# A weight buffer of the expert down products lent to the gathered rows: two buffers in place of three

## The reference, cut to what matters

```
q = (xc @ w_q).reshape(128, 8, 2, 128)              # a block of 128 tokens
s = einsum("chsd,hskd->chsk", q, keys)              # 8 heads, 2 x 128 keys
... top 16 of each side, then the best 16 pairs: 16384 experts, 16 picked by each of 8 heads
e = i1 * 128 + i2;  g = softmax(best_s)
act = gelu(einsum("cd,chkd->chk", xc, u_tab[e]))
out = einsum("chk,chkd->cd", g * act, v_tab[e])
x = x + g_f * out
```

## Time and profile before

| | us |
|---|---|
| median of 3 runs (lowest, highest) | 2940.29 (2937.99, 2942.69) |
| the profiled execution, its own time | 2935.12 |
| its span, first to last instruction | 2933.3 |

### The profile page before, as it was taken

One profiled execution on the slowest core, in us unless ns is written; L12 is line 12 of the kernel. 1 busy time (PEld: TensorE's weight loads), 2 busy tenths in 40 slices (PEclk: granted clock), 3 DMA queues, 4 the chain that ended last, 5 costly groups with the idle time before them and its releaser, 6 DMA issues. The chain is left out here.

```text
span 2933.3 us, 36691 instructions
## 1 busy us (share of the span) xinstructions
PE 2632.2 (90%) x12550; PEld 2159.5 (74%) x12550; DVE 1990.6 (68%) x4287; ACT 1043.5 (36%) x2939; POOL 1349.4 (46%) x1076
## 2 busy tenths in 40 slices
PE   4789889999999999999965888999999999999992
PEld 2544558888888888888854766888888887878881
DVE  2356249998877866666674247998877775666667
ACT  3335142269878700000004423229888830000000
POOL 0000034455666666666550005365666674655562
PEclk7889999999999999999987989999999999999996
DMA  7247133799999999999991223599999999999995
GB/s 304 65 189 303 43 116 130 289 384 380 356 410 409 409 404 409 409 409 409 409 375 57 86 71 117 207 374 366 360 384 409 407 407 404 409 409 409 409 409 212
DMA packets 246591, 917.87 MB, mean 313 GB/s; under 512 B 27120, under 2 KB 32272, under 8 KB 239120
## 3 DMA queue, kind: packets, MB, share of 16 engines
q0 software_dynamic: 147456, 536.94, 46.6%
q1 hardware_dynamic: 94800, 374.54, 33.1%
q10 hardware_dynamic: 4160, 4.19, 0.4%
HBM read 909.27 MB, written 6.29 MB: 312 GB/s over the span
## 5 line engine op out<-in xcount | busy, mean ns | idle before, releaser
L1199 PE MATMUL exp_down<-peer_gates,all_ring 128*128 128x256 f32 x2720 | 613.3, 382 | 22.3 <-DMA all_ring<-in_peer_v 22.3
L1172 PE MATMUL exp_out<-peer_both,all_ring 128*128 128x256 f32 x2752 | 617.4, 380 | 9.4 <-DMA all_ring<-in_uT 5.7
L1199 PEld LDWEIGHTS exp_down<-peer_gates,all_ring 128*128 128x128 f32 x2720 | 508.0, 190 | 117.1 <-DMA all_ring<-in_peer_v 50.5
L1172 PEld LDWEIGHTS exp_out<-peer_both,all_ring 128*128 128x128 f32 x2752 | 515.9, 190 | 83.1 <-DMA all_ring<-in_uT 11.8
L1090 POOL DMA_INDIRECT all_xT<-in_u_rows,peer_eidx x278 | 350.4, 1260 | 169.6 <-DVE peer_dots L1548 115.6
L1555 DVE SCALAR_TENSOR_TENSOR peer_both<-all_xT,peer_dots,peer_both 128x1024 f32<-128x1024 f32 x226 | 290.3, 1285 | 147.7 <-DMA all_xT<-in_peer_v,peer_eidx 144.1
L1548 DVE CUSTOM_DVE_ANT_0 all_xT<-all_xT,peer_both 128x1024 f32<-128x1024 f32 x278 | 338.1, 1222 | 66.9 <-DMA all_xT<-in_u_rows,peer_eidx 65.2
L1063 POOL TENSOR_TENSOR ask_w_lo<-all_ring,ask_w_hi 128x1024 fp32r<-128x1024 f32 x22 | 52.5, 2390 | 675.4 <-ACT ask_w_hi L1227 675.4
L1090 POOL DMA_INDIRECT all_xT<-in_peer_v,peer_eidx x230 | 271.3, 1180 | 176.8 <-DVE peer_both L1555 144.3
L1199 PE MATMUL exp_down<-peer_gates,spare_ring 128*128 128x256 f32 x1376 | 315.6, 382 | 13.9 <-DMA spare_ring<-in_peer_v 13.9
L1299 ACT ACTIVATE spare_heavy<-all_iota_b,spare_index 128x128 f32<-128x128 bf16 x1024 | 314.2, 411 | 0.0
(11 more groups left out here) (288 smaller groups left out, 3843.0 us busy)
## 6 DMA issues: line engine op xcount, KB each, us to landing
all_ring<-in_uT SPq DMA_DIRECT2D x172, 512.0 KB, 6.8
all_ring<-in_peer_v SPq DMA_DIRECT2D x170, 512.0 KB, 6.8
mix_raw<-in_ada_tiles SPq DMA_DIRECT2D x48, 1024.0 KB, 9.6
spare_ring<-in_peer_v SPq DMA_DIRECT2D x86, 512.0 KB
spare_ring<-in_uT SPq DMA_DIRECT2D x84, 512.0 KB
all_ring<-in_w_peer_q SPq DMA_DIRECT2D x22, 512.0 KB, 3.7
all_ring<-in_w_gs_in SPq DMA_DIRECT2D x16, 512.0 KB, 3.7
all_ring<-in_w_in SPq DMA_DIRECT2D x12, 512.0 KB, 3.7
```

Of the source, the lines that this page charges most:

```text
L1172: mm = nc.tensor.matmul(outs[:, c % 2, 0:DENSE], raw[c % R][:, k, :], hd[:, k, :], start=(k == 0), stop=(k == KD - 1))
L1199: mm = nc.tensor.matmul(dn[:, m, :], raw[at % R][:, m, :], gates[:, :, c, :], start=(c == 0 and m % 2 == 0), stop=(c == NKEYS - 1), skip_g ...
```

## The change

The v chunks go through two buffers, `raw[0]` and `raw[1]`, and the third, `raw[2]` (`q.ring`), becomes a tenth place for gathered rows from slot NEAR + 2 = 264 on. The ups keep three buffers. The load of v chunk c waits for down c - 2, and the first two wait for the last up that read their buffer (`last_up` is 126, 127 and 125 for the three buffers). The first fetch into the new place waits for up 125.

```diff
-        R = len(raw)
+        R, DOWN = len(raw), 2
+        last_up = [max(range(j, NKEYS, R)) for j in range(R)]
...
+        rows += [raw[DOWN][:, :, :].rearrange("p k n -> p (k n)")]
+        spans += [(NEAR + 2, SLOTS)]
         rows += [x[:, :] for x in q.late]
...
-        ROW, OWN, PICKED_ROW = 4, 5 + len(EARLY), 6 + len(EARLY)
+        ROW, OWN, PICKED_ROW, RING_ROW = 4, 5 + len(EARLY), 6 + len(EARLY), 7 + len(EARLY)
...
-            for c in range(2 * NKEYS):
+            for c in range(NKEYS):
...
-                if c < NKEYS:
-                    sp.dma_start(raw[c % R][:, :, :], t["uT"][l][c]).then_inc(s_in[c % R], 16)
-                else:
-                    sp.dma_start(raw[c % R][:, :, :].rearrange("p k n -> p (k n)"),
-                                 v_dram[l * NKEYS + c - NKEYS]).then_inc(s_in[c % R], 16)
+                sp.dma_start(raw[c % R][:, :, :], t["uT"][l][c]).then_inc(s_in[c % R], 16)
+            for c in range(NKEYS):
+                j = c % DOWN
+                sp.wait_ge(s_mm, NKEYS + c - DOWN + 1 if c >= DOWN else last_up[j] + 1)
+                sp.dma_start(raw[j][:, :, :].rearrange("p k n -> p (k n)"), v_dram[l * NKEYS + c]).then_inc(s_in[j], 16)
...
+                elif j == RING_ROW:
+                    pool.wait_ge(s_mm, last_up[DOWN] + 1)
...
             def down(c):
-                at = NKEYS + c
-                pe.wait_ge(s_in[at % R], 16 * (at // R + 1))
+                j = c % DOWN
+                pe.wait_ge(s_in[j], 16 * (last_up[j] // R + 1 + c // DOWN + 1))
...
-                    mm = nc.tensor.matmul(dn[:, m, :], raw[at % R][:, m, :], gates[:, :, c, :],
+                    mm = nc.tensor.matmul(dn[:, m, :], raw[j][:, m, :], gates[:, :, c, :],
```

## The result

The changed kernel takes 3262.07 us (median of 5 runs, 3259.55 to 3268.61), the kernel before 2937.99 us beside it: 1.1106 times as long (95% interval 1.109 to 1.1121), 324 us slower. The forecast was 3205 us with a range of 3110 to 3245: the direction held, and the size did not. Of the mechanism one term was mis-sized, what a fall of TensorE's clock costs.

A forecast was written before the change was run, and what follows sets the result against it. The prediction took DMA bytes to bound the downs' stage; downs of 5.97 us beside rows, then 3.72 us, add 138 us a layer, 275 us on 2935.1, giving 3210, 3215 for the median, taken as 3205 us, range 3110 to 3245.

The forecast's parts named there:

- The bound of before: In the downs' stretch of the kernel before, DMA bytes bind: chunks and rows together take 402 of 408 GB/s.
- The landing stays: With two buffers, a v chunk beside rows still lands in about 7.0 us (median 6.8 before).
- Rival C: Downs beside rows: the landing shrinks to 5.0 us, a down takes 4.37 us, total 3029 us; chance 0.11.
- E: Downs beside rows: landing falls to 4.1 us, stage stays bound by bytes, not slower, 2931 us; chance 0.04.
- the estimate of 4.4 us: A chunk's landing beside rows by the Trainium skill's transfer cost at half the rate: 4.4 us, total near 2971 us.
- D: Downs beside rows: landing grows to 7.9 us, with clock falls a down takes 6.42 us, total 3241 us; chance 0.12.
- rival B: Downs beside rows: the clock stays at 2.4 GHz, a down takes 5.37 us, total 3160 us; chance 0.21.
- The clock: TensorE's clock falls after most pauses beside rows, 1.2 us each, 0.6 us a down, making 5.97 us a down.
- a bound, 3.5 us: Upper limit on a clock fall's cost per pair of downs: 7.07/2 = 3.5 us, all at half the clock.
- The rows: Gathered v rows beside the slowed chunks take 1.67 us each in place of 2.02, done near 1465 us.
- The tenth place: The new row place lets 10 rows be out in place of 9, keeping the queue full, with no other worth.
- near 0.85: Sign to look for: TensorE's granted clock well under 1.00 in the stretch with rows, and 1.00 after it.

The follow-up runs named there:

- e7: Kernel before with four chunk buffers for the downs and eight row places: 1.0021 of the kernel before, 6 us slower.
- e6: Kernel before, three chunk buffers kept, with a tenth row place from slot 290 on in freed gates memory: 1.0002 of the kernel before.
- e1: Changed kernel with 7 extra matmul calls on resident data after each second down while c < 80: 1.0816 of the kernel before, 3173 us.
- e11: Changed kernel without the gathers of v rows, two chunk buffers: 0.9934 of the kernel before, 2920 us.
- e3: Changed kernel with the tenth row place taken away, two chunk buffers, the third left empty: 1.1087 of the kernel before.
- e9: Kernel before, three chunk buffers and nine row places, with v chunks loaded in halves of 2 KB per partition: 1.0065 of the kernel before.
- e5: Changed kernel with each v chunk loaded in quarters of 128 KB, each asked for after its quarter of the down: 1.1033 of the kernel before.

## Why the prediction was wrong, point by point

**The bound of before: right.** e7 takes all idle time from TensorE and gains nothing; e6 adds a place and gains nothing. The stage is bound by the DMA's bytes (408 GB/s in all three).

**The landing stays: right.** 6.8 us with one or two chunks out, where the kernel before has two nearly always; the mean beat of e1 is 10.9 us against 10.74. Rival C (5.0), whose chunk has the queue to itself, and E (4.1) fall with it, and so does the estimate of 4.4 us from the Trainium skill ("DMA: Bandwidth & Descriptors", Anatomy of one DMA); its figures are for transfers that GpSimd issues, while SyncE issues these. D (7.9) falls too: its 3241 us would have come nearer than the forecast, but by a landing that didn't come. The landing part of the loss was put at 225 us (rival B) and e1 measured some 240: T was 5.46 in place of 5.37, and the downs after the rows took 3.81 in place of 3.72 (e11 shows 3.88 with no rows at all).

**The clock: the term that failed.** The step that failed is "a fall after most pauses, at 1.2 us each". The falls came (in 23 of 25 beats); their price was wrong. It was taken from one pause in the trace of before. Of the 32 matmuls priced there, begun at 2119.68, only what ran until 2122.19 ran at the low clock: 2.5 us of work, which at half speed costs 1.2 us. In the beat shown above it is 6.3 us of work (1303.53 to 1309.80), and the price is 10.2 - 7.07 = 3.1 us. Over the stretch, T of 6.55 less 5.46 in e1 makes 1.09 us a down or 2.2 us a pair, where 0.6 and 1.2 were forecast. The working had a bound, 3.5 us, and used it neither for the value nor for the range. (If both downs ran wholly at half the clock, a pair would take 7.07 us more; the 3.5 are for the first down, the one in the chain.) With the bound, T is 7.12 and the same formulas give 3278 us, so a range that reached there would have held the result.

With T = 6.55 as measured, the working's own formulas give rows of 1.63 us that end at 415 us, 63 downs done and 65 x 3.72 = 242 us more: 657 in place of 639, and 2 x 157 = 313 us in all. With the measured 3.81 us for the later downs they give 325 us, and 324 were measured. The clock's part was put at 50 us and measured as 85 (changed kernel less e1). That is the larger part of the miss; the landing's 15 us comes next. The 10 us taken off at the end, from 3215 to 3205, because not every pause would cost 1.2 us, went the wrong way.

Why the clock stays low for 6.8 us after most pauses and for 3.4 us after others isn't settled. Rows 8 and the beat shown don't differ in what TensorE did in the first 3.4 us of low clock (busy 2.92 of 3.42 us there, 2.87 of 3.40 here), and the changed kernel has both lengths. The Trainium skill ("TensorE: Matmul & The Clock Gate", HAM oscillation) describes the pattern, a fall at each wait for data; the trace agrees in 23 of 25 beats, and the price of a fall had to be measured.

**The rows: right.** 1.67 us were forecast, 1.64 measured; they ended at about 1456 us against 1466. The tenth place was costed at nothing, and e3 and e6 show so, within 0.4% and 0.2%.

**What would have shown it.** The forecast named a clock "near 0.85"; it was 0.79. That line points to the term, and the 10.2 us of two downs give its size.

## What to carry to other kernels

A ring of n buffers covers a load of length L only if n - 1 uses of a buffer last at least L, with L taken from the stage in which the load runs beside its neighbours: 6.8 us here, and 3.7 in a quiet stage. Where a lost buffer makes TensorE pause, ask how much work follows each pause before you take over the price of a fall of its clock from another place, and let the range reach to the bound. And a third of a scarce memory given to a stream that was not short of places buys nothing: ask each stream what ends its waits (bytes, here) before giving it room.

## What the runs showed that was not expected

Useless work made the kernel faster: 7 matmul calls in each pause took the ratio from 1.1106 to 1.0816, and the clock then stayed at 1.00.

Beside rows of 4 KB per partition, the chunks got 131 GB/s in pieces of 2 KB (e9) and 77.5 in pieces of 1 KB (e5), one piece for each piece of a row. In pieces of 4 KB they got 152 GB/s (e7, 524.3/3.45) without being short. By the same count half of the rate would be open to them there, which no run shows. The Trainium skill says that a DMA engine takes turns between its queues by packet ("DMA: Bandwidth & Descriptors", Queues, rings and completion order); the two runs agree as far as they go (how many pieces one turn moves, no run shows), and show the price: who cuts a transfer finer gets less. A landing hardly shrinks with the size (6.8 us for 512 KB, 6.3 for 256 KB), nor with the number of row places (6.7 with six).
